# One hybrid S5, attention and PEER layer on one core: TensorE's order inside a slot of the expert loop

## What is computed

```
q = (hc @ w_query).reshape(TOKEN_CHUNK, PEER_HEADS, 2, PEER_HALF)
s = jnp.einsum('thpd,pkd->thpk', q, sub_keys)
s1, i1 = lax.top_k(s[:, :, 0], PEER_TOPK)
s2, i2 = lax.top_k(s[:, :, 1], PEER_TOPK)
cand = s1[..., :, None] + s2[..., None, :]
top_s, top_c = lax.top_k(cand, PEER_TOPK)
idx = e1 * PEER_N_KEYS + e2
g = jax.nn.softmax(top_s, axis=-1)
u = expert_down[idx]
a = jax.nn.gelu(jnp.einsum('thkd,td->thk', u, hc))
return jnp.einsum('thk,thkd->td', g * a, expert_up[idx])
```

## Time and profile before

| what | value |
|---|---|
| median of three executions | 3142.93 us |
| lowest and highest | 3140.16 and 3144.03 us |
| span of the profiled execution, first to last instruction | 3137.4 us |
| TensorE busy, weight loads | 2320.7 us (74%), 1911.3 us (61%) |
| VectorE, ScalarE, GpSimd busy | 2218.5, 2031.0, 1292.2 us |
| moved by DMA | 1162.55 MB, of it 1077.61 MB by the gathers |
| mean DMA rate, granted TensorE clock | 371 GB/s, 0.789 |

### The profile page before, as it was taken

One profiled execution on the slowest core, in us unless ns is written; L12 is line 12 of the kernel. 1 busy time (PEld: TensorE's weight loads), 2 busy tenths in 40 slices (PEclk: granted clock), 3 DMA queues, 4 the chain that ended last, 5 costly groups with the idle time before them and its releaser, 6 DMA issues.

```text
span 3137.4 us, 38315 instructions
## 1 busy us (share of the span) xinstructions
PE 2320.7 (74%) x13074; PEld 1911.3 (61%) x13074; DVE 2218.5 (71%) x5295; ACT 2031.0 (65%) x3762; POOL 1292.2 (41%) x1165
## 2 busy tenths in 40 slices
PE   3989877888786976677666667777767666777666
PEld 2665556777674655666566666666666555666555
DVE  8983558888894776777776666667667767767654
ACT  3214338888785665777667667676676666766665
POOL 1001224444443443545444444445444444444443
PEclk9989988988887986786777776667676777676766
DMA  7600359999999999999999999999999999999997
GB/s 258 196 31 1 123 221 420 420 377 370 384 403 418 419 418 420 421 421 421 419 421 401 421 421 421 410 422 421 418 417 416 421 416 419 410 421 420 420 421 327
DMA packets 175460, 1162.55 MB, mean 371 GB/s; under 512 B 22720, under 2 KB 23632, under 8 KB 43808
## 3 DMA queue, kind: packets, MB, share of 16 engines
q0 software_dynamic: 148352, 1077.61, 83.2%
q1 hardware_dynamic: 26224, 80.39, 6.8%
q10 hardware_dynamic: 688, 2.10, 0.2%
HBM read 1147.32 MB, written 11.53 MB: 369 GB/s over the span
## 4 chain that ended last, share of the span: by engine, by line
DMA 35%; DVE 24%; PE 15%; ACT 9%; issue 4%; POOL 1%; POOLq 0%; DVEq 0%; ACTq 0%
DMA pair<-in_experts_dram,idx_g 35%; DVE pair L1776 12%; PE acc_a L1440 5%; ACT pair L1575 4%; PE pef L1415 3%; PE acc_b L1440 2%; POOL pair L1275 1%; ACT w L1573 1%; ACT L1571 1%; DVE top_i L1704 1%; DVE staged L1705 1%; PE pef L1339 1%; DVE top_i L1707 1%; DVE top_v L1706 1%; PE acc_b L1320 1%
## 5 line engine op out<-in xcount | busy, mean ns | idle before, releaser
L1275 POOL DMA_INDIRECT pair<-in_experts_dram,idx_g x1024 | 1227.5, 1199 | 1418.0 <-PE acc_a L1440 795.0
L1776 DVE SCALAR_TENSOR_TENSOR pair<-pair,h 128x1024 f32<-128x1024 f32 x1024 | 1247.7, 1221 | 678.8 <-DMA pair<-in_experts_dram,idx_g 677.1
L1575 ACT ACTIVATE pair<-pair,w 128x1024 f32<-128x1024 f32 x1024 | 1176.3, 1149 | 33.4
L1440 PE MATMUL acc_a<-ident,pair 128*128 128x128 f32 x5120 | 863.5, 330 | 379.7 <-ACT pair L1575 373.9
L1440 PEld LDWEIGHTS acc_a<-ident,pair 128*128 128x128 f32 x5120 | 731.4, 172 | 502.8 <-ACT pair L1575 476.1
L1440 PE MATMUL acc_b<-ident,pair 128*128 128x128 f32 x3072 | 588.2, 359 | 295.9 <-ACT pair L1575 295.6
L1440 PEld LDWEIGHTS acc_b<-ident,pair 128*128 128x128 f32 x3072 | 484.6, 186 | 392.1 <-ACT pair L1575 387.2
L1571 ACT ACTIVATE ga<-a 128x1 f32<-128x1 f32 x1024 | 204.3, 199 | 685.4 <-DVE pair L1776 680.5
L1573 ACT ACTIVATE w<-ga,g 128x1 f32<-128x1 f32 x1024 | 301.6, 295 | 33.2
L1415 PE MATMUL pef<-h2t,wq 128*128 128x128 f32 x1536 | 203.7, 297 | 0.0
L1415 PEld LDWEIGHTS pef<-h2t,wq 128*128 128x128 f32 x1536 | 202.8, 216 | 1.0 <-issue 1.0
(11 more groups left out here) (344 smaller groups left out, 2295.3 us busy)
## 6 DMA issues: line engine op xcount, KB each, us to landing
wada<-in_w_ada_t_dram SPq DMA_DIRECT2D x48, 512.0 KB, 5.3
pair<-in_experts_dram,idx_g POOLq DMA_INDIRECT x1024, 16.3
pieces<-in_w_query_t_dram SPq DMA_DIRECT2D x16, 512.0 KB, 10.1
wq<-in_w_query_t_dram SPq DMA_DIRECT2D x4, 2048.0 KB, 33.6
wout_a<-in_w_out_dram SPq DMA_DIRECT2D x1, 4096.0 KB, 13.1
x2s<-out_dram SPq DMA_DIRECT2D x8, 512.0 KB, 12.0
out_dram<-h SPq DMA_DIRECT2D x8, 512.0 KB, 8.7
wout_b<-in_w_out_dram SPq DMA_DIRECT2D x1, 4096.0 KB, 34.7
```

Of the source, the lines that this page charges most:

```text
L1275: p.indirect_dma_start(pair[n % R], None, A["experts"], bass.IndirectOffsetOnAxis(ap=idx[:, t % (2 * PH), k:k + 1], axis=0)).then_inc(pair ...
L1440: last = t.matmul(accs[ACC[i]][:, k * P:(k + 1) * P], pair[n % R][:, D + k * P:D + (k + 1) * P], S.ident[:], is_transpose=True, start=n % ...
L1575: s_.activation(pair[n % R][:, D:], pair[n % R][:, D:], ACT.Copy, scale=w[:, n % NA:n % NA + 1]).then_inc(scaled, 1)
L1776: v.scalar_tensor_tensor(down, down, 1.0, h2[:, n // P, :], ALU.mult, ALU.mult, accum_out=a[:, n % NA:n % NA + 1]).then_inc(dotted, 1)
```

## The change

In TensorE's loop two steps move from the end of the slot's list to its head, turn_back with its condition and add_up. Nothing is added or removed, no slot number, wait or buffer is changed, and no other engine's list is touched.

```diff
             for n in range(SLOTS):
+                if n - 2 in END:
+                    turn_back(END[n - 2])
+                add_up(n)
                 if n in AT_SCORES:
                     at_scores(AT_SCORES[n])
                 if n in AT_BACK:
...
                 if n in SCORED:
                     scores(SCORED[n])
-                if n - 2 in END:
-                    turn_back(END[n - 2])
-                add_up(n)
             turn_back(NT - 1)
```

## The result

The changed kernel takes 3198.93 us (median of four executions, 3195.2 to 3215.63), the kernel before 3143.48 us on the same chip. The ratio is 1.0185, 95% interval 1.0162 to 1.0208: slower by some 55 us. The forecast was slower, 3154 us with a range to 3178; the measured time lies outside it.

What follows compares the result with a forecast made beforehand. The prediction took transfers to bound the late stage and VectorE's list to bound 640 to 940 us. Span 3137.4 + 14 (attention) - 3 (turn_back) = 3148.4 us, plus 5.5 around it, gave 3154 us, range 3134 to 3178.

Steps and rivals of the forecast that it cites:

- The limit: Transfers bound 1230 to 3110 us (DMA share 1.01); VectorE's list bounds 640 to 940 us (busy 263.58 of 300 us).
- landed rows were no use sooner: In 640 to 940 us, buffers freed 1 to 4 us sooner taken at 0; upper end 18 us.
- The attention pieces, 640 to 940 us: Each piece comes one add_up later and VectorE waits longer: 19 us plus a third of 32, 29 us, halved to +14.
- the next piece then comes with slack again: In 640 to 940 us, a wait stopping VectorE also stops ScalarE, so the 29 us was halved to +14 us.
- The same shift in 500 to 600 us costs nothing: Early loop: transfers are full, so a few us of VectorE's delay only shorten its wait for landings; 0 us.
- the ring's cover: Late-stage gathers take 16.6 us against 5.5 least delayed; the 11 us queue hides buffer delays smaller than that.
- The projection, taken at 0: In 940 to 1230 us, six rows later delay some gathers 1 to 2 us; 0, or 12 us without cover.
- The queue covers it: In 940 to 1230 us, queued transfers hide GpSimd issuing some gathers 1 to 2 us later; 0 us.
- turn_back, -3 us: In slot 131 it goes ahead of scores and values, for which VectorE had waited 4.45 us; -3 us.
- The 5.5 us around the span: Added to the 3148.4 us span, since the median shown before was that much over the span.
- clearly slower: Pieces behind unscaled rows keep all their delay, 51 us less 3: up to 3191 us, milder form 3169; chance 0.10.
- no change: VectorE's extra waits cancel: within 6 us (0.2%), 3137 to 3149 us, in the middle 3143; chance 0.30.

## Why the prediction was wrong in size

The sum had 14 - 3 = 11 us; by slot 18 + 27 + 11 + 1 = 57 us were lost. Two stages put at nothing and one term halved make the difference. Point by point:

- **The limit.** Right for the late stage, which is bound by transfers: slots 264 to 1023 lost 1 us, the late queries nothing that can be told (3144.94 us with them behind), though ScalarE's waits grew from 23 to 68 us. Right also in that VectorE's list and its waits for TensorE set the early stage, with one thing missing: TensorE's clock, which took back the 3.5 us of turn_back. That landed rows were no use sooner also held: rows first with the readers' slack restored gave no gain.
- **The attention pieces, 640 to 940 us.** The direction and mechanism were right and the term was mis-sized. It was put at 29 us and then halved, as "the next piece then comes with slack again". The halving is the step that failed: slots 64 to 190 lost 27 us, near the 29 before it. An explanation, argued and not tested: the piece that VectorE needs next is held behind a row that itself hangs on VectorE's last dot product, so a wait moves the next piece too. VectorE's waits for pieces grew from 23 to some 53 us in that window, not to 40, and the DMA share fell to 0.90. The sum took a row at 1.04 us, its length at the upper level of the clock, and had no term for TensorE being busy 15.5 us longer with the same work.
- **"The same shift in 500 to 600 us costs nothing: the DMA share is 1.01 there."** This step failed as well, with 18 us in slots 0 to 64 against nothing. The share told that transfers were full, and VectorE's waits for landings, 27.8 us in these slots, looked like room; the gathers took 15.7 us in the median there, much as in the late stage, so the ring's cover looked the same too. But VectorE waited 29 us more for turns and for copies of scores, and only 9 us of landings made way. The wide queries, which the prediction does not mention, are a large part of it: with them and attention's pieces behind it is 18.2 us at slot 64, with the wide queries alone 12.2, with attention alone 9.6.
- **The projection, taken at 0 with 12 us "without that cover".** It cost the 12: by slot 11 us, by the run with the projection alone put back 13. The step that failed is "The queue covers it". VectorE's wait at L1678 went from 5.0 to 24.2 us, and the DMA share of slots 215 to 264 fell from 1.01 to 0.97. Why the queue covered ScalarE's waits later and not these was not taken apart.
- **turn_back, -3 us.** It was gained at its place and gone 27 slots further; the sum should have had 0.
- **The 5.5 us around the span.** A time and its span differ by 2 us (3196.28 and 3194.3 us, and likewise in every run here); the other 3.5 us are the profiled execution's distance from the median. The sum is the same either way.

What the runs put in place of 3154: attention alone 34 us (measured alone), projection 13 or 10 (in front without and with attention), and 10 for all query and turn pieces (3153.04 less 3143.28), the late ones at most some 4 of them by the medians. Together 54 to 57 us, against 55 measured; each of these has an interval of several us, so that they fit may in part be luck. The rival called clearly slower came nearest, with pieces that keep all of their delay; its chance of 0.10 was too small, and its upper end, 3191 us, is still 8 us short, as it has nothing before slot 64. The rule from the Trainium skill's page Perfetto Trace Analysis, section Identifying the Most-Contended Engine, would have made it no change, as DMA was the most contended engine of the whole run; the measurement decides against using it across stages. The same page's section Optimization Strategy allows for that: it says that a kernel can have several regimes with different most contended engines. The port ceiling of 435 GB/s, from the Trainium skill's page DMA: Bandwidth & Descriptors, section Where 436 GB/s comes from, was not reached in the full windows shown here; they stayed at 418 to 419 GB/s.

## What to carry to other kernels

In an in-order list where pieces stand between items that wait for data, ask what the engine does while it waits: a piece in front of the waiting item is done during the wait, the same piece behind it comes later by the wait and its own length. Price a shift by the slack of its readers, engine by engine, and take a full transfer queue as cover at most up to the time that the readers spend waiting for it; in slots 0 to 64 only a third of that time gave way. Compare stages by slot and look at the granted clock beside the waits, since pieces behind a longer wait may also run slower. If a list must be shifted, shift the readers by the same amount: here that brought back 44 of 56 us.

## What was not expected

That the wide queries would count, that the projection's readers wait in one place for 12.8 us, and that a real gain of 3.5 us is taken away 27 slots later by TensorE's clock. One row more of delay cost 34 us, two rows 79. Scores alone in front gave back 14 us, turn and values alone 13, both together 36; whether that gap is real the intervals leave open.
